# Latent heads: the softmax sums' reciprocals move from the probabilities to the products with V, and the retention transfers are issued by two engines

## What is computed

```
q = (rms_norm(c_q, q_norm) @ w_uq).reshape(B, S, H, QK_NOPE_DIM + QK_ROPE_DIM)
kv = (rms_norm(c_kv, kv_norm) @ w_ukv).reshape(B, S, H, QK_NOPE_DIM + V_HEAD_DIM)
...
s = q_nope . k_nope + q_pe . k_pe
p = jax.nn.softmax(s * MLA_SCALE, axis=-1)
return jnp.einsum('bhqk,bkhd->bqhd', p.astype(v.dtype), v)
```

## Time and profile before

| | |
|---|---|
| median of 3 runs | 1026.31 us (1025.63 to 1026.74) |
| the profiled execution's own time | 1026.88 us |
| its span, first to last instruction | 1025.1 us |
| PE busy | 1015.6 us, 99% of the span |
| DVE, ACT, POOL busy | 686.6, 564.4, 140.7 us |
| mean granted TensorE clock | 0.998 of full speed |

### The profile page before, as it was taken

One profiled execution on the slowest core, in us unless ns is written; L12 is line 12 of the kernel. 1 busy time (PEld: TensorE's weight loads), 2 busy tenths in 40 slices (PEclk: granted clock), 3 DMA queues, 4 the chain that ended last, 5 costly groups with the idle time before them and its releaser, 6 DMA issues.

```text
span 1025.1 us, 14271 instructions
## 1 busy us (share of the span) xinstructions
PE 1015.6 (99%) x4764; PEld 836.6 (82%) x4764; DVE 686.6 (67%) x1041; ACT 564.4 (55%) x923; POOL 140.7 (14%) x219
## 2 busy tenths in 40 slices
PE   9999999999999999999999999999999999999997
PEld 6999888888877778888888888888887688888886
DVE  6777865646688985656568565656788785655643
ACT  6665654545567764444556454454676854454542
POOL 1001450000143253000014000000400221000002
PEclk9999999999999999999999999999999999999999
DMA  9574567566643467657576665757653455756551
GB/s 369 187 243 168 195 222 240 183 221 206 207 144 125 145 226 251 224 195 239 180 232 195 231 214 191 244 175 243 200 184 124 146 184 182 245 184 231 195 168 46
DMA packets 109694, 204.61 MB, mean 200 GB/s; under 512 B 57472, under 2 KB 62992, under 8 KB 109648
## 3 DMA queue, kind: packets, MB, share of 16 engines
q1 hardware_dynamic: 107472, 198.55, 57.9%
q0 software_dynamic: 1888, 5.17, 1.6%
q10 hardware_dynamic: 288, 0.31, 0.1%
HBM read 187.20 MB, written 1.05 MB: 184 GB/s over the span
## 4 chain that ended last, share of the span: by engine, by line
PE 93%; DVE 3%; DMA 1%; ACT 1%; SPq 1%; POOL 0%; issue 0%; POOLq 0%; DVEq 0%; ACTq 0%
PE pG L2185 16%; PE pG L2177 16%; PE pG L2181 16%; PE pD L2177 11%; PE pD L2181 11%; PE pD L2185 11%; PE pG L2158 2%; PE pG L2160 1%; PE pG L2164 1%; PE pT L2194 1%; DVE w_low L1735 1%; DMA h<-in_x 1%; PE pD L2158 1%; PE pD L2164 1%; PE pD L2160 1%; PE pT L2379 1%
## 5 line engine op out<-in xcount | busy, mean ns | idle before, releaser
L1735 DVE TENSOR_TENSOR w_low<-raw,w_high 128x1024 fp32r<-128x1024 f32 x339 | 408.9, 1226 | 181.4 <-ACT w_high L1424 171.3
L1424 ACT ACTIVATE w_high<-raw 128x1024 fp32r<-128x1024 f32 x340 | 353.5, 1056 | 192.1 <-PE pG L2185 134.4
L2177 PE MATMUL pG<-w_high,xTh 128*128 128x512 f32 x712 | 219.8, 390 | 0.0
L2185 PE MATMUL pG<-w_low,xTh 128*128 128x512 f32 x712 | 219.4, 389 | 0.2 <-DVE w_low L1735 0.2
L2181 PE MATMUL pG<-w_high,xTl 128*128 128x512 f32 x712 | 219.3, 389 | 0.0
L2185 PEld LDWEIGHTS pG<-w_low,xTh 128*128 128x128 f32 x712 | 133.6, 188 | 28.3 <-DVE w_low L1735 0.6
L2181 PEld LDWEIGHTS pG<-w_high,xTl 128*128 128x128 f32 x712 | 133.5, 188 | 28.0 <-DVE xTl L1795 0.2
L2177 PEld LDWEIGHTS pG<-w_high,xTh 128*128 128x128 f32 x712 | 133.2, 188 | 27.5
L1531 ACT ACTIVATE gate<-pG,stat 128x256 f32<-128x256 f32 x102 | 48.4, 474 | 151.8 <-PE pG L2185 135.9
L2177 PE MATMUL pD<-w_high,aTh 128*128 128x512 f32 x348 | 107.8, 391 | 0.0
L2181 PE MATMUL pD<-w_high,aTl 128*128 128x512 f32 x348 | 107.4, 390 | 0.1
(11 more groups left out here) (318 smaller groups left out, 1113.0 us busy)
## 6 DMA issues: line engine op xcount, KB each, us to landing
raw<-in_stream SPq DMA_DIRECT2D x340, 512.0 KB, 4.3
aF<-aB SPq DMA_DIRECT2D x320, 32.0 KB, 2.5
post<-in_posts POOLq DMA_DIRECT2D x5, 512.0 KB, 5.9
early<-in_stream SPq DMA_DIRECT2D x4, 512.0 KB, 12.5
xF<-hg SPq DMA_DIRECT2D x32, 64.0 KB, 2.5
xF<-hg POOLq DMA_DIRECT2D x32, 64.0 KB, 2.2
h<-in_x SPq DMA_DIRECT2D x2, 512.0 KB, 11.6
first_w<-in_opening SPq DMA_DIRECT2D x2, 384.0 KB, 4.2
```

The lines of the kernel that those rows point to most:

```text
L1424: sc.activation(w_high[:, slot(static):slot(static) + CHUNK], raw_of(static), ACT.Copy).then_inc(w_high_done, 1)
L1735: ve.tensor_tensor(w_low[:, slot(static):slot(static) + CHUNK], raw_of(static), w_high[:, slot(static):slot(static) + CHUNK].bitcast(F32), ...
L2177: pe.matmul(dst, ah, w_high[:, where:where + n], start=start, stop=False)
L2185: mm = pe.matmul(dst, ah, w_low[:, where:where + n], start=False, stop=stop)
```

## The change

The probabilities are no longer divided. `MN` is gone: `MPT` turns the raw exponentials, and the division is made on the products with V. They stand with heads and features on partitions and tokens in columns, so the reciprocals must be turned too. The new step `ML(t)` does it: POOL raises the eight sums of a row block to the power -1 and copies each to 64 columns (`weights_wide`, 128x512), PE turns that in four transposes into the free half of the other row block's `pD`, ACT copies it to `heads_cat[t]`. `MAT(t)` is now one DVE product of `pD[t]` and `heads_cat[t]`, and `CAT(t)` the split into `xTh` and `xTl` that `MAT` was before.

The transfers of `RV` are issued by SP (parts a = 0, 1) and POOL (a = 2, 3), and `RV(1)` stands earlier in the last turn. `MPV` comes behind the projection of its turn. `decay(2)` moves from turn 6 to the end of turn 7.

```diff
     for v in range(1, 8):
-        step("MN", v - 1)
         step("MS", v)
         if v in (1, 3):
             refill(step, freed, 1)
         step("ME", v)
+        if v == 7:
+            step("RV", 1)
+        project(*beside.pop(0))
         if v in (3, 5, 7):
             step("MPV", v - 3)
             step("MPV", v - 2)
-        project(*beside.pop(0))
         step("MPT", v - 1)
         if v == 2:
             step("VC", 0)
         if v == 4:
+            step("ML", 0)
             step("RV", 0)
             step("RROPE", 1, 1)
         if v == 5:
+            step("MAT", 0)
             step("RSUM",)
             step("RB", 1, 0)
         if v == 6:
             step("RB", 1, 1)
         if v == 7:
-            step("RV", 1)
             step("VC", 1)
-        if v in (2, 4, 6):
-            step("decay", v // 2 - 1)
-    step("MN", 7)
+        if v in (2, 4, 7):
+            step("decay", v // 2 - 1 if v < 7 else 2)
     refill(step, freed, 2)
     project(4, 1, 1)
     step("MPT", 7)
-    step("MAT", 0)
+    step("ML", 1)
+    step("CAT", 0)
     step("gate", 0)
...
     refill(step, freed, 1)
+    step("MAT", 1)
     project(4, 1, 3)
...
     output(0, 1)
-    step("MAT", 1)
+    step("CAT", 1)
...
             def RV(t, ph):                                    # SP
                 sp.wait_ge(ms_psum, 4 * (t + 1))
+                if t == 1:
+                    sp.wait_ge(rT_moved, 64)
...
-                    for a in range(4):
+                    for a in range(0, 2):
...
+            def ML(t, ph):                                    # POOL
+                pool.wait_ge(mp_ready, 8 * (t + 1))
+                if t == 1:
+                    pool.wait_ge(wide_psum, 1)
+                link(pool.tensor_tensor(lrec[t][:, 0:MLA_HEADS], lsum[t][:, 0:MLA_HEADS], one_neg[:, 0:MLA_HEADS], ALU.pow))
+                pool.tensor_copy(weights_wide[:].rearrange("p (a f) -> p a f", f=HD),
+                                 lrec[t][:, 0:MLA_HEADS].unsqueeze(2).broadcast_to([P, MLA_HEADS, HD])).then_inc(wide_ready, 1)
...
+            def RV(t, ph):                                    # POOL
+                pool.wait_ge(ms_psum, 4 * (t + 1))
+                if t == 1:
+                    pool.wait_ge(rT_sent, 64)
+                for part in range(2):
+                    pool.wait_ge(rB_ready, 2 * t + part + 1)
+                    for a in range(2, 4):
...
+            def ML(t, ph):                                    # ACT
+                sc.wait_ge(wide_psum, t + 1)
+                if t == 1:
+                    sc.wait_ge(rT_moved, 64)
+                    sc.wait_ge(rT_sent, 64)
+                sc.activation(heads_cat[t], pD[1 - t][:, 512:1024], ACT.Copy).then_inc(wide_copied, 1)
+
+            def CAT(t, ph):                                   # ACT
                 x_product(sc, 4, t)
-                sc.wait_ge(mpv_done, 4 * (t + 1))
-                sc.activation(xTh[t][:, 0:4, :].rearrange("p k r -> p (k r)"), pD[t][:, 512:1024], ACT.Copy).then_inc(cath_ready[t], 1)
+                sc.wait_ge(cat_ready, t + 1)
+                sc.activation(xTh[t][:, 0:4, :].rearrange("p k r -> p (k r)"), heads_cat[t], ACT.Copy).then_inc(cath_ready[t], 1)
...
             def MAT(t, ph):                                   # DVE
+                ve.wait_ge(mpv_done, 4 * (t + 1))
+                ve.wait_ge(wide_copied, t + 1)
+                ve.tensor_tensor(heads_cat[t], pD[t][:, 512:1024], heads_cat[t], ALU.mult).then_inc(cat_ready, 1)
+
+            def CAT(t, ph):                                   # DVE
                 ve.wait_ge(cath_ready[t], 1)
...
             def MPT(v, ph):                                   # PE
-                pe.wait_ge(mn_ready, v + 1)
+                pe.wait_ge(mp_ready, 2 * (v + 1))
...
+            def ML(t, ph):                                    # PE
+                pe.wait_ge(wide_ready, t + 1)
+                if t == 1:
+                    pe.wait_ge(cat_ready, 1)
+                for j in range(4):
+                    mm = turned(pD[1 - t][:, 512 + P * j:512 + P * (j + 1)], weights_wide[:, P * j:P * (j + 1)])
+                mm.then_inc(wide_psum, 1)
+
             def MPV(v, ph):                                   # PE
                 t, j = v // 4, v % 4
+                if v == 4:
+                    pe.wait_ge(cat_ready, 1)
...
             def RS(i, ph):                                    # PE
-                    for t in range(2):
-                        pe.wait_ge(rT_moved[t], 128)
+                    pe.wait_ge(rT_moved, 128)
+                    pe.wait_ge(rT_sent, 128)
...
             def Oc(t, kt, ph):                                # PE
                 if kt == 0:
                     pe.wait_ge(rgate, t + 1)
+                    pe.wait_ge(cat_ready, 2)
```

More of the change, by code:

```diff
@@ L812, in build @@
         post = place("post", [P, D], F32)
+        weights_wide = place("weights_wide", [P, 512], F32, at[0])
+        heads_cat = [place("heads_cat", [P, 512], F32, at[0] + 2048)[:], post[:, 0:512]]
         junk = [place(f"junk{t}", [P, D], BF16) for t in range(2)]
@@ L1185, in RV @@
                 sp.wait_ge(ms_psum, 4 * (t + 1))
+                if t == 1:
+                    sp.wait_ge(rT_moved, 64)
                 for part in range(2):
                     sp.wait_ge(rB_ready, 2 * t + part + 1)
-                    for a in range(4):
+                    for a in range(0, 2):
                         dst = rkT[:, t, :, a, :] if part else rqT[:, t, a, :, :]
-                        sp.dma_start(dst, block_turned(t, part)[32 * a:32 * a + 32, :]).then_inc(rT_moved[t], 16)
+                        sp.dma_start(dst, block_turned(t, part)[32 * a:32 * a + 32, :]).then_inc(rT_moved, 16)
             def finish(ph):
@@ L1399, in finish @@
                 pool.tensor_tensor(rr[1], ms[1], half_neg[:, 0:1], ALU.pow).then_inc(end_weights, 1)
-            steps = {f.__name__: f for f in (start, parts, squares, rest, norm, early_tables, second_low, spread, reload, finish, tail, rope, S, LAT, VC, decay, GNvar)}
+            def RV(t, ph):
[5 more added lines that the diff above has]
+                    for a in range(2, 4):
+                        dst = rkT[:, t, :, a, :] if part else rqT[:, t, a, :, :]
+                        pool.dma_start(dst, block_turned(t, part)[32 * a:32 * a + 32, :]).then_inc(rT_sent, 16)
+            steps = {f.__name__: f for f in (start, RV, parts, squares, rest, norm, early_tables, second_low, spread, reload, finish, tail, rope, S, LAT, ML, VC, decay, GNvar)}
             in_loop = ("G", "D", "T", "Y", "R")
@@ L1714, in _ @@
             steps = dict(start=start, exp_table=exp_table, silu_table=silu_table, high=high, R=refill, turn=turn, parts=parts, squares=squares, gain=gain, norm=norm, second=second, finish=finish,
-                         weigh=weigh, tail=tail, G=G, T=T, Y=Y, proj=proj, QKT=QKT, E=E, PT=PT, AT=AT, X=X, LAT=LAT, U=U, MT=MT, ME=ME, MPT=MPT, decay=decay, gate=gate_r, silu=silu, MAT=MAT, SQ=SQ, RY=RY)
+                         weigh=weigh, tail=tail, G=G, T=T, Y=Y, proj=proj, QKT=QKT, E=E, PT=PT, AT=AT, X=X, LAT=LAT, U=U, MT=MT, ME=ME, MPT=MPT, decay=decay, gate=gate_r, silu=silu, ML=ML, CAT=CAT, SQ=SQ, RY=RY)
             walk(sc, lambda name, *a, ph=None: steps[name](*a, ph) if name in steps else None)
@@ L2068, in U @@
                 wide = [x.unsqueeze(1).broadcast_to([P, 8, half]) for x in turns(t)]
-                rotate(mq[:, :, NOPE:NOPE + half], mq[:, :, NOPE + half:QK], *wide, u_tmp()).then_inc(mqk_ready[t], 1)
+                rotate(mq[:, :, NOPE:NOPE + half], mq[:, :, NOPE + half:QK], *wide, u_tmp()).then_inc(mqk_ready, 1)
             def MT(t, ph):
@@ L2083, in MS @@
                 ve.tensor_scalar(negm[t][:, 2 * j:2 * j + 2], mx[t][:, 2 * j:2 * j + 2], MLA_SCALE, None, ALU.mult).then_inc(mmax_ready, 1)
[L2085 to L2091, removed]
             def VC(t, ph):
@@ L2145, in _ @@
             steps = dict(start=start, low=low, R=refill, opening=opening, low_half=low_half, turn=turn, parts=parts, second=second, second_low=second_low, spread=spread, gain=gain, rest=rest, finish=finish, tail=tail, join=join, G=G, V=V, T=T, Y=Y,
-                         rope=rope, QKT=QKT, S=S, N=N, AT=AT, LAT=LAT, KPE=KPE, U=U, RROPE=RROPE, RSUM=RSUM, MT=MT, MS=MS, MN=MN, VC=VC, RB=RB, RM=RM, GNvar=GNvar, GNout=GNout,
-                         MAT=MAT, RY=RY, RL=RL)
+                         rope=rope, QKT=QKT, S=S, N=N, AT=AT, LAT=LAT, KPE=KPE, U=U, RROPE=RROPE, RSUM=RSUM, MT=MT, MS=MS, VC=VC, RB=RB, RM=RM, GNvar=GNvar, GNout=GNout,
+                         MAT=MAT, CAT=CAT, RY=RY, RL=RL)
             walk(ve, lambda name, *a, ph=None: steps[name](*a, ph) if name in steps else None)
@@ L2477, in MT @@
             def MT(t, ph):
-                pe.wait_ge(mqk_ready[t], 2)
+                pe.wait_ge(mqk_ready, 2 * t + 2)
                 for i, src in enumerate((mq, mk)):
@@ L2576, in _ @@
```

(2 more changed lines are left out.)

15 lines of the change are left out of this document (8 added, 7 removed).

## The result

The kernel after takes 1032.37 us (median of four runs, 1032.24 to 1033.73) against 1026.03 for the kernel before on the same chip (four runs, 1025.63 to 1026.74): a ratio of 1.0066, 95% interval 1.0053 to 1.0078. It is slower by 6.3 us as medians; the profiled executions are 1032.24 and 1026.88, 5.4 apart, and their spans 1030.4 and 1025.1.

What follows compares the result with a forecast made beforehand. PE was taken as the bound, busy 99% of the span. The terms -1.0 + 0.9 + 1.5 + 4.1 - 1.0 + 0.6 = +5.1 on the profiled 1026.88 give 1032.0, 1031.4 as a median; range 1027.8 to 1033.9.

Steps and rivals of the forecast that it cites:

- the rival with the falling clock: PE's stall of over 4 us drops the clock, half pace costs 1.7 us: +6.8 in all, 1033.1; chance 0.18.
- Products behind the projection: `MPV` behind its turn's projection: PE no longer waits for ACT's copy and loses less between kinds of products; -1.0.
- New transposes: `ML` adds four transposes twice on PE, 2 x 0.44 = +0.88 us.
- The wait of `ML(0)`: PE stalls for POOL's first weights, power 2.55 and copy 1.04 us: +1.5, bounds no stall to 2.9.
- The wait of `ML(1)`: PE stalls for the second weights, behind ACT's copy, `decay(2)` and POOL's power and copy: +4.1, bounds 2.2 to 5.2.
- The sentence that POOL's part of the transfers does not add: At `ML(1)`: POOL's four issues and `VC(1)` are done some 0.9 before the decays arrive, so they add no stall.
- The transfers: SP and POOL issue four each, a projection earlier; PE's wait ahead of the first retention scores goes: -1.0.
- The later split: `Oc(0,0)` now waits for `MAT(1)` too, stalling PE: +0.6, bounds 0 to 1.0.
- The rule that was weighed: POOL's power at twice DVE's price, some 0.3 us: sum +1.3, 1027.6; as a rival, chance 0.07.

Runs made afterwards that it cites:

- experiment 5: Kernel after with `MAT(1)` ahead of DVE's weight split: first kernel with DVE making the weights, 1026.98 us; second with POOL making the second weights first, 1027.73 us.
- experiment 1: Kernel after with `decay(2)` put back at its old place, the end of turn 6: 1033.45 us, ratio 1.0073.
- Experiment 4: Kernel after with POOL making the second row block's weights ahead of `VC(1)` and `decay(2)`: 1028.68 us, ratio 1.0024.
- experiment 6: Kernel before, division kept, with moves alone: products with V behind the projection plus earlier, split transfers 1025.34 us; products alone 1025.19; transfers alone 1025.87.
- experiment 3: Kernel after with both row blocks' weights made by DVE (reciprocal and copy) in place of POOL: 1029.40 us, ratio 1.0032.
- experiment 2: Kernel after with twelve unused products of 512 columns on PE ahead of its wait for the second weights: 1030.87 us, ratio 1.0045.
- experiment 7: Kernel after with DVE making the weights and SP issuing all eight transfers of each row block: 1027.90 us, ratio 1.0023.

## Why the prediction was right, and where its steps were off

The forecast of 1031.4 and its sign were right, 1.0 under the median; the rival with the falling clock, 1033.1, lies 0.7 above it, and the clock did fall. Step by step, on PE from the first latent to the first retention scores; times between starts, in which a wait with its hand-over counts:

1. *Products behind the projection*, -1.0 predicted: -0.72. From unit 3's scores to unit 4's PE needs 3.86 (779.53 to 783.39) against 4.45 (779.21 to 783.66), 0.59 less, and turns 5 and 7 give 0.06 and 0.07. The prediction took unit 4's start from the chain of waits (783.83), 0.17 later than the timeline's 783.66: part of the gain was a difference between views.
2. *New transposes*, +0.88: right; in the first kernel of experiment 5, where nothing waits, four of them take 0.44.
3. *The wait of `ML(0)`*, +1.5: 0.30 of idle time, 0.5 between starts. Power and copy took 1.77 and 0.83 where 2.55 and 1.04 were summed; the longer of two rows was the wrong choice here. The hand-overs, put at 0.1 without a row, were 0.12 (785.60 to 785.66 and 786.49 to 786.55).
4. *The wait of `ML(1)`*, +4.1: 3.65 of idle time, 3.8 between starts. The prediction's count from unit 6's transposes to the weights was 5.9 us; it took 5.7 (797.37 to 803.09), with a power of 1.66 (2.55 predicted) and a copy of 1.59 (1.04), two errors that for the most part cancel. The chain over ACT's copy and `decay(2)` was the last releaser in this kernel, as POOL's 0.68 of idle time before the product shows. But it ended only these 0.68 behind POOL's own queue, and experiment 1 shows that putting `decay(2)` back shortens nothing. The sentence that POOL's part of the transfers does not add was true only because both ways are about equally long. Experiment 4 shows that the order on POOL is the cause: with only the weights moved ahead of `VC(1)` and `decay(2)`, the waits fall to 0.8 in all. Of the 3.1 by which the second one falls, `decay(2)` with its wait for ACT is 1.1 (798.63 to 799.72).
5. *The transfers*, -1.0: right against this profiled execution, in which the wait of 1.03 is gone. But it was a poor thing to count on. In the kernel before the slowest of the eight transfers landed after 3.6 us, with a median of 2.2 (the last is issued at 798.6, and 798.6 + 3.6 is 802.2, where PE's wait ends); with the products alone moved (experiment 6), issued by the same engine at the same place, after 2.4 at most, and nothing waited. So the wait came with one late transfer rather than with the eight issues. That most executions of the kernel before have no such wait would fit three things: its profiled execution is 0.85 above the median of the four runs; experiment 5's first median is 1.3 above that of the kernel before at an equal stage; and the transfers alone (experiment 6) shorten the stage by 1.1 against this profile but leave the median where it was (1025.87 against 1025.79). It would also account for the 1.0 by which the forecast fell short, since the term of -1.0 was then taken off a median that did not hold the wait. But no run here shows an unprofiled execution's waits: it stays argued.
6. *The later split*, +0.6: nothing in this kernel, since the 13.55 us behind the retention scores equal the 13.56 before. PE was held back 5 us while DVE and ACT were not, so `MAT(1)` was ready. Once the wait of `ML(1)` was removed the stop was 2.0 and 1.3 (experiments 3 and 4), both over the upper bound of 1.0. The sum had added two stalls of which the first covers the second.
7. *The clock*, a rival with 0.18: it came true, on top of the forecast, with 1.36 measured (experiment 2) where 1.7 was worked out. The prediction had taken its absence as the likelier, on a gap of some 4 us; that step was wrong. The price was worked out from the first matmuls of the kernel, which run at half pace although the profile gives the granted clock there as 1.00; the trace doesn't settle that.

Together -0.72 + 0.88 + 0.5 + 3.8 - 1.03 + 1.36 = 4.8, the 4.83 measured. So the total of +5.1 was right partly by luck: `ML(0)` and the later split were 1.6 too dear in sum, and the clock, left out, cost 1.4.

*The rule that was weighed.* POOL's power took 1.66 to 1.77 on 128x8 in the kernel after, and DVE's reciprocal of the same sums 0.20 (experiment 3). The factor of two of the Trainium skill (GPSIMD Engine Reference, Engine selection), which would have given +1.3, does not hold for this pair of operations: the rows show eight to nine. It is stated for additions, products and maxima, and a power is none of these. Its advice, elementwise work to VectorE, is borne out: experiment 3's weights were ready before PE asked.

What the change itself is worth once its waits are gone: the first kernel of experiment 5 has a stage of 45.5, experiment 6's with the division and both moves 43.8. The difference of 1.6 is the eight transposes (0.44 and 0.47 between the scores around them) and 0.7 between the second and the third retention scores (804.74 to 809.14 against 803.85 to 807.52), 0.43 of it PE's wait ahead of the retention products. Nothing is left over as a gain: the removed division buys nothing here, as DVE was not the bound.

## What to carry to other kernels

Before work is moved to a lightly used engine, read that engine's queue at the place, not its share of the span: POOL was 15% busy, and the weights came 3.7 us late because three other steps stood ahead of them. Moving work off an engine with slack won nothing here, and each operation that it added to the bounding engine was paid in full. Add stalls with care: a long one hides a later one, which comes back when the first is mended, and compare a profiled execution with the median of its kernel before you count on a wait that it shows: it may be that execution's own.

## What the hardware showed unexpectedly

- In these profiles the granted clock fell to 1.2 GHz after single idle times of PE of 3.65 (after), 4.0 (experiment 1), 1.99 (experiment 3) and 1.9 us (experiment 7), and stayed at 2.4 GHz through 1.3 (experiment 4), 1.03 (before) and 0.9 (experiment 2), with PE busy on both sides in each case; no profile has an idle time between these two groups. In the kernel after it cost 1.36 us, in experiment 3 1.57: nearly as much as the shorter stop itself.
- The fall does not come at a fixed time behind PE's last work. In the kernel after it came during the wait; in experiments 1, 3 and 7 only when PE had been at work again for 1.0, 0.6 and 1.5 us (from 803.31, 808.94 and 808.52 to 804.3, 809.5 and 810.0). One stretch of each of the three in this order, PE busy throughout; the clock is the third number from the end, and its mean gives the moment of the fall:

```profile
804.00:805.00 1.00, 1.00 (x4) 0.81 (x3) 0.00 (x0) 1.00 (x2) 0.00 (x0) 0.65 0.44 156
...
809.00:810.00 1.00, 1.00 (x4) 0.81 (x5) 1.00 (x4) 1.00 (x2) 0.47 (x1) 0.77 0.71 184
...
809.00:810.00 1.00, 1.00 (x5) 0.58 (x4) 1.00 (x4) 1.00 (x2) 0.07 (x1) 0.99 1.00 328
```

- POOL's copy of the same 128x512 took 0.61, 0.83 and 1.59 us, and its power on 128x8 1.66, 1.77 and 2.67. The sum of both is 2.60 and 2.28 for the two row blocks of experiment 4, and 3.25 and 3.28 where a product of POOL stands directly ahead (second row block of after and of experiment 1), so the pair is the better figure than either row. What makes the difference no run shows.
- DVE's copy of 128x512 took 0.43 us for the first row block and 0.90 for the second, in the same kernel.
